# A two-layer hybrid block on one core: the low-rank part of the next RWKV chunk computed in the tail of the chunk before, with reordered norms and a split constants load

## What is computed

```python
h  = rms_norm(x) * norm1_w * (1 + scale) + shift         # scale, shift: silu(c) @ ada_w + ada_b
p  = h @ w_in
# RWKV-7 part; columns of p: r, k, v (512 each), decay and a (64 per direction), gate (128)
p  = p + mu * (neighbour_mean(p) - p)                     # mixing with neighbours in the sequence or grid
g  = sigmoid(gd) @ g_up
kk = k*k_k / norm(k*k_k)
for d in 0, 1:
    w   = -softplus(-(w0[d] + tanh(wd) @ w_up[d])) - 0.5  # low rank: "zw"
    a   = sigmoid(a0[d] + ad @ a_up[d])                   # low rank: "za"
    k_d = k * (1 + (a - 1) * k_a)
o  = forward and backward delta-rule scan(r, w, k_d, v, kk, a)
y1 = (group_norm(o) * lnx_w + lnx_b + sum(r * (k_0 + k_1) * r_k) * v) * g
x += gate1 * (sum of three gated branches) @ w_out        # the others: retention, HGRN2
x += gate2 * (relu(h2 @ w1)**2) @ w2                      # h2: rms_norm(x), scaled and shifted
```

## Time and profile before

| | |
|---|---|
| runs | 2445.9, 2450.27, 2450.76 us (median 2450.27) |
| the profiled execution | 2445.06 us, of which the span from first to last instruction is 2443.3 us |
| mean granted TensorE clock | 0.953 of full speed |
| busy | PE 2190.7 us (90%), DVE 1338.5, ACT 972.3, POOL 421.2 |
| shares of the chain that ended last | PE 76%, DVE 14%, ACT 4%, issue 3%, DMA 1%, POOL 1% |

### The profile page before, as it was taken

One profiled execution on the slowest core, in us unless ns is written; L12 is line 12 of the kernel. 1 busy time (PEld: TensorE's weight loads), 2 busy tenths in 40 slices (PEclk: granted clock), 3 DMA queues, 4 the chain that ended last, 5 costly groups with the idle time before them and its releaser, 6 DMA issues.

```text
span 2443.3 us, 50283 instructions
## 1 busy us (share of the span) xinstructions
PE 2190.7 (90%) x21274; PEld 1849.4 (76%) x21274; DVE 1338.5 (55%) x1913; ACT 972.3 (40%) x1369; POOL 421.2 (17%) x395
## 2 busy tenths in 40 slices
PE   5988889898999899989999988888888889898998
PEld 1655768677778688868888867677776878897998
DVE  3345665656466634454444465476576545566666
ACT  3534232333354323333323346343343364445544
POOL 1001322313134300010000010142232246100000
PEclk8998999999999999989999989899999989898999
DMA  6522412224111123322232223200000022355553
GB/s 248 209 101 76 157 62 106 96 80 157 62 52 61 61 95 99 134 69 95 98 101 95 95 104 132 80 28 28 11 20 27 12 81 70 106 184 173 179 177 128
DMA packets 64447, 241.33 MB, mean 99 GB/s; under 512 B 7136, under 2 KB 8288, under 8 KB 62816
## 3 DMA queue, kind: packets, MB, share of 16 engines
q1 hardware_dynamic: 62064, 218.66, 26.3%
q10 hardware_dynamic: 2160, 19.46, 2.0%
HBM read 231.80 MB, written 6.29 MB: 97 GB/s over the span
## 4 chain that ended last, share of the span: by engine, by line
PE 76%; DVE 14%; ACT 4%; issue 3%; DMA 1%; POOL 1%; DVEq 0%; ACTq 0%; POOLq 0%; SPq 0%
PE psum L392 17%; PE psum L393 16%; PE psum L394 16%; PE psum L447 10%; PE psum L456 2%; PE psum L767 2%; DMA weight_ring<-in_weights 1%; PE psum L703 1%; PE psum L424 1%; PE psum L425 1%; PE psum L485 1%; PE psum L426 1%; DVE work L1155 1%; DVE weight_ring_parts L968 1%; PE psum L434 1%
## 5 line engine op out<-in xcount | busy, mean ns | idle before, releaser
L392 PE MATMUL psum<-normed_high,weights_high 128*128 128x512 f32 (+1 forms) x1592 | 582.9, 366 | 25.5 <-DVE weight_ring_parts L968 12.6
L393 PE MATMUL psum<-normed_low_part,weights_high 128*128 128x512 f32 (+1 forms) x1592 | 566.3, 356 | 0.0
L394 PE MATMUL psum<-normed_high,weight_ring_parts 128*128 128x512 f32 (+1 forms) x1592 | 565.3, 355 | 0.0
L968 DVE TENSOR_TENSOR weight_ring_parts<-weight_ring,weights_high 128x1024 fp32r<-128x1024 f32 (+1 forms) x327 | 411.3, 1258 | 273.5 <-ACT weights_high L1460 266.4
L1460 ACT ACTIVATE weights_high<-weight_ring 128x1024 fp32r<-128x1024 f32 (+1 forms) x327 | 339.9, 1039 | 190.8 <-PE psum L394 136.7
L392 PEld LDWEIGHTS psum<-normed_high,weights_high 128*128 128x128 f32 x1592 | 311.1, 195 | 85.8 <-issue 27.7
L393 PEld LDWEIGHTS psum<-normed_low_part,weights_high 128*128 128x128 f32 x1592 | 311.3, 196 | 41.0 <-issue 3.9
L394 PEld LDWEIGHTS psum<-normed_high,weight_ring_parts 128*128 128x128 f32 x1592 | 310.7, 195 | 40.4
L447 PE MATMUL psum<-work 64*64 64x64 f32 (+1 forms) x7040 | 243.1, 224 | 30.4 <-issue 10.7
L447 PEld LDWEIGHTS psum<-work 64*64 64x64 f32 x7040 | 232.9, 135 | 48.6 <-issue 35.8
L392 PE MATMUL psum<-hidden_high,weights_high 128*128 128x512 f32 (+1 forms) x512 | 172.4, 337 | 3.7 <-DVE hidden_low L1407 3.7
(11 more groups left out here) (233 smaller groups left out, 3534.7 us busy)
## 6 DMA issues: line engine op xcount, KB each, us to landing
weight_ring<-in_weights SPq DMA_DIRECT2D x407, 512.0 KB, 3.5
x_scratch<-work ACTq DMA_DIRECT2D x2, 2048.0 KB, 8.4
weight_ring<-in_weights SPq DMA_DIRECT2D x16, 256.0 KB, 2.7
work<-x_scratch ACTq DMA_DIRECT2D x2, 2048.0 KB, 8.9
work<-in_ret_constants ACTq DMA_DIRECT2D x2, 1152.0 KB, 13.2
work<-in_x ACTq DMA_DIRECT2D x1, 2048.0 KB, 14.0
constants<-in_constants ACTq DMA_DIRECT2D x1, 1317.5 KB, 8.3
work<-in_small_weights ACTq DMA_DIRECT2D x1, 1152.0 KB, 5.2
```

Source lines behind the costliest of these rows:

```text
L392: mm(ps, w[0][:, cols], x[0], start=first, stop=False)
L393: mm(ps, w[0][:, cols], x[1], start=False, stop=False)
L394: return mm(ps, w[1][:, cols], x[0], start=False, stop=last)
L968: tt(ring_r[:, i % RING, o], ring[:, i % RING, o], high[:, n % HIGHS, o].bitcast(F32), ALU.subtract).then_inc(vec_split.sem, vec_split.ste ...
```

## The change

Start and norms:

- the constants load is split: 75 + 512 columns are loaded after x at the start, the other 2048 columns (the masks, a semaphore of their own) after the first norm
- in layer 0 ACT squares x before it copies the modulation rows, PE sums the squares before it makes the modulation columns, and the split of four weights is spread (two before the tiles, one behind tile 1, one behind tile 3)
- in every norm the last square isn't added by DVE: PE sums it in a second accumulating matmul
- in the norms 1 and 2 the high parts of tiles 0 and 1 are written by ACT in an activation of their own instead of by POOL
- the small derived vectors of layer 1 are made in layer 0's last MLP quarter
- `modulation_columns(0, 1)` moves from retention to behind the small projections

RWKV:

- chunk c + 1's low-rank products move into the tail of chunk c on PE, direction 0 in front of the mean's sum and direction 1 between mean and bonus; their sigmoids and exponentials move with them on ACT, their scans and a factors on DVE to between mean and bonus
- `decayed(c + 1)`, five products, ends chunk c on DVE; a times decay comes there from POOL
- chunk 0 has no tail before it: there DVE does `low_rank_parts(0)` and `decayed(0)` before `mix` of k
- the edge columns go from DVE to ACT
- the low part of v's weights moves behind the products with k
- v's projection always uses bank 1 (`second`)

```diff
-                eng.wait_ge(vec_norm.sem, vec_norm.at("squares added", l, which, KT - 1))
-                mm(ps[:, 0:t1 - t0], ones, work[:, TN + 2560:TN + 2560 + t1 - t0], start=True, stop=True).then_inc(
+                eng.wait_ge(vec_norm.sem, vec_norm.at("squares added", l, which, KT - 2))
+                mm(ps[:, 0:t1 - t0], ones, work[:, TN + 2560:TN + 2560 + t1 - t0], start=True, stop=False)
+                eng.wait_ge(act_norm.sem, act_norm.at("square", l, which, KT - 1))
+                mm(ps[:, 0:t1 - t0], ones, work[:, TN + 512:TN + 512 + t1 - t0], start=False, stop=True).then_inc(
...
                 if l == 0:
+                    norm(l, 1)
                     modulation_columns(0, 0)
-                    norm(l, 1)
...
                     if c == 0:
                         eng.wait_ge(act_rwkv.sem, act_rwkv.at("small ready", l))
-                    for d in range(2):
-                        low_rank(c, d)
+                        for d in range(2):
+                            low_rank(c, d)
...
-                    project(big, big_filled, split("rw", l, c, 2), ("rkv", l, c, 2))
+                    project(second, big_filled, split("rw", l, c, 2), ("rkv", l, c, 2))
...
+                    if c < NT - 1:
+                        low_rank(c + 1, 0)
                     eng.wait_ge(vec_rwkv.sem, vec_rwkv.at("o summed", l, c))
                     sum_over(bones, wk(RW_SCR)[:, lo:N], ("mean", l, c), w)
+                    if c < NT - 1:
+                        low_rank(c + 1, 1)
                     eng.wait_ge(vec_rwkv.sem, vec_rwkv.at("bonus terms", l, c))
                     sum_over(bones, wk(RW_KS)[:, lo:N], ("bonus", l, c), w)
...
+                def low_rank_parts(c):
+
+                    for d in range(2):
                         eng.wait_ge(act_rwkv.sem, act_rwkv.at("decay sigmoid", l, c, d))
                         G, sg, msk = wk(RW_D[d] + LT), wk(RW_D[d] + WW), kcol(K_SCAN, N)
...
+                    for d in range(2):
+                        B = RW_D[d]
+                        eng.wait_ge(act_rwkv.sem, act_rwkv.at("a sigmoid", l, c, d))
+                        ts(wk(B + KTI), wk(B + BT), pcol(l, "ka", c), dcol(D_OMKA + c), ALU.mult, ALU.add).then_inc(vec_rwkv.sem, vec_rwkv.step())
...
+                def decayed(c):
+
+                    tt(ks, wk(RW_D[0] + KTI)[:, lo:N], wk(RW_D[1] + KTI)[:, lo:N], ALU.add).then_inc(vec_rwkv.sem, vec_rwkv.step())
...
+                        tt(wk(B + BT), wk(B + BT), wk(B + ABT), ALU.mult).then_inc(vec_rwkv.sem, vec_rwkv.step())
...
+                        tt(wk(B + KTI), wk(B + KTI), wk(B + ABT), ALU.mult).then_inc(vec_rwkv.sem, vec_rwkv.step())
...
+                low_rank_parts(0)
+                decayed(0)
+                for c in range(NT):
...
                         tt(wk(B + KTI), wk(B + KTI), k, ALU.mult).then_inc(vec_rwkv.sem, vec_rwkv.step())
                         eng.wait_ge(vec_rwkv.sem, vec_rwkv.n)
+                    weights_low(split_at["rw", l, c, 2] + 1)
                     mix(c, r, ("mixed", l, c))
...
+                    if c < NT - 1:
+                        low_rank_parts(c + 1)
                     eng.wait_ge(big_filled.sem, big_filled.at("bonus", l, c))
...
-                    weights_low(split_at["rw", l, c, 2] + 4)
+                    if c < NT - 1:
+                        decayed(c + 1)
+                    else:
+                        weights_low(split_at["rw", l, c, 2] + 4)
...
+                        if k < 2:
+                            act(normed_hi[:, k, u0:u1], work[:, o + u0 - t0:o + u1 - t0], ACT.Identity,
...
+                    if c < NT - 1:
+                        tables(SIGMOID)
+                        low_rank(c + 1, 0)
+                        low_rank(c + 1, 1)
+                        tables(LOG_EXP)
                     eng.wait_ge(big_filled.sem, big_filled.at("var", l, c))
...
+                    if c < NT - 1:
+                        decays(c + 1)
+                    else:
+                        tables(SIGMOID)
```

More of the change, by code:

```diff
@@ L284, in banks @@
             return Banks(psum, first, n, width, steps, known, loaded_vectors, held)
-        big, first = banks(0, 4), banks(0, 1)
+        big, first, second = banks(0, 4), banks(0, 1), banks(1, 1)
         wide = banks(2, 1, 2)
@@ L1156, in decay_sums @@
                         eng.wait_ge(vec_rwkv.sem, vec_rwkv.n)
-                    mix(4 + c, k, ("mixed", l, 4 + c))
-                    ts(wk(RW_KK), k, pcol(l, "kk", c), None, ALU.mult).then_inc(vec_rwkv.sem, vec_rwkv.step(("kk raw", l, c)))
-                    eng.wait_ge(vec_rwkv.sem, vec_rwkv.n)
-                    for d in range(2):
-                        decay_sums(d)
                     for d in range(2):
@@ L1464, in _, with squares @@
             split_high = [0]
-            def norm(l, which):
+            def squares(l, which):
                 t0, t1 = (0, N) if which == 1 or l < L - 1 else (NC, N)
@@ L1485, in norm @@
                     eng.wait_ge(act_norm.sem, act_norm.n)
+            def norm(l, which):
+                t0, t1 = (0, N) if which == 1 or l < L - 1 else (NC, N)
+                if which == 3:
+                    t0 = NC
+                n = t1 - t0
                 eng.wait_ge(out_filled.sem, out_filled.at("squares summed", l, which))
@@ L1490, in norm @@
                     return
-                eng.wait_ge(vec_cond.sem, vec_cond.at("vectors derived", l) if which == 1 else vec_cond.at("norm scale", l, "n2"))
+                if (l, which) == (0, 1):
+                    weights_high(2)
+                eng.wait_ge(vec_cond.sem, vec_cond.at("norm scale", l, "n1" if which == 1 else "n2"))
                 ws, sh = (D_WS1, 0) if which == 1 else (D_WS2, 24)
@@ L1501, in norm @@
                         eng.wait_ge(act_norm.sem, act_norm.n)
+                    if (l, which) == (0, 1) and k in (1, 3):
+                        weights_high(3 + k // 2)
                 act_norm.also(("h", l, which))
@@ L1527, in _ @@
                 lo, w, m0 = first_query(l)
-                act(dcol(D_LG, 8), pcol(l, "dec", 0, 8), ACT.Exp).then_inc(act_cond.sem, act_cond.step(("ret decay exp", l)))
-                eng.wait_ge(act_cond.sem, act_cond.n)
                 if l == 0:
+                    act(dcol(D_LG, 8), pcol(l, "dec", 0, 8), ACT.Exp).then_inc(act_cond.sem, act_cond.step(("ret decay exp", l)))
+                    eng.wait_ge(act_cond.sem, act_cond.n)
+                    squares(0, 1)
                     modulation_rows(0, 0)
-                    weights_high(HIGHS)
                 norm(l, 1)
@@ L1663, in _ @@
                     rsqrt(act_rwkv, wk(RW_SQ), big.get("kk norm", l, c), 1.0, "l2", ("kk rms", l, c), ("drained", "kk norm", l, c))
+                    eng.wait_ge(vec_rwkv.sem, vec_rwkv.at("kk ready", l, c))
+                    for d in range(2):
+                        e = 0 if d == 0 else 63
+                        act(chunks(RW_D[d] + KR, 1, e, 128), chunks(RW_KK, 1, e), ACT.Copy).then_inc(act_rwkv.sem, act_rwkv.step(("edges", l, c, d)))
+                        eng.wait_ge(act_rwkv.sem, act_rwkv.n)
                     project(2)
@@ L1839, in _ @@
                             weights_high(split_at["m2", l, q, f] + HIGHS)
+                if l < L - 1:
+                    act(dcol(D_LG, 8), pcol(l + 1, "dec", 0, 8), ACT.Exp).then_inc(act_cond.sem, act_cond.step(("ret decay exp", l + 1)))
+                    eng.wait_ge(act_cond.sem, act_cond.n)
+                    squares(l + 1, 1)
+            squares(L - 1, 3)
             norm(L - 1, 3)
```

112 lines of the change are left out of this document (63 added, 49 removed).

## The result

The changed kernel takes 2429.03 us (median of four runs, 2426.62 to 2431.42) against 2449.69: a ratio of 0.9923, 95% interval 0.9909 to 0.9936. That is faster by 20.7 us where I had forecast 40.

What follows compares the result with a forecast made beforehand. PE, busy 90% of the span, was taken as the bound. Terms 22.3 + 12.3 - 8.9 + 9.6 + 2.7 + 2.3 = 40.3 us off 2445.06 gave 2404.8; with 5.2 for the median, 2410, range 2394 to 2432.

Steps and rivals of the forecast that it cites:

- PE's wait for the edge columns: PE before the first Gram product of each RWKV chunk: 38.3 us in eight waits, forecast gone in chunks 1 to 3.
- new waits for POOL's square: PE's kk sum would wait about 1.4 us in layer 0, 3.8 in layer 1, 6.5 in chunks 0.
- These lose: Chunk 0, low rank and decay before `mix` of k: loss of 4.2 us in layer 0, 4.7 in layer 1.
- The start and the columns: Start: 9.6 us gained by shorter loads and path; modulation columns moved out of retention: 2.7 gained.
- The first L424: At the start, PE would go on at 42.6 us instead of 53.01.
- I count these as equal: Layer 1, chunks 1 to 3: clock cost 2.7 in kk and v against 2.4 gained at Gram products, leaving 12.3 us.
- the product of the bonus terms, which I put into a gap: DVE at level 2: the product fits in a gap and costs nothing; without the gap 0.7 us a chunk, 5.6 in all.
- v and the modulation end at 356.3: Layer 0, chunk 1: PE's own queue sets the first Gram product at 356.3 instead of 361.05, gaining 4.75 us.
- 2.7 us of clock "I take": Layer 0, chunks 1 to 3: full clock at Gram product and transposes gains 2.7 us a chunk, bounds 0 and 2.7.
- Only the waits go, the clock doesn't come back: Rival, 20%: chunks 1 to 3 win 14.2 us in layer 0, 4.5 in layer 1, total 24.4, so 2426.
- The rule against the change: Moved scans beside POOL's square make var about 0.9 us later, at no cost; without slack 5.4 us worse.
- the norms, 2.3: Norms: net gains 0.7 before layer 0's MLP, 0.2 before layer 1, 1.4 before the last MLP, 0 at the end.

Runs made afterwards that it cites:

- the run with k first: Changed kernel, but in chunk 0 DVE mixes k and makes its keys before the scans, a factors and decay products: 2406.81 us, ratio 0.9839 to the kernel before.
- keep_busy: Changed kernel plus PE products whose result is thrown away, filling the wait before the sum of squared keys: ratio 0.9859 to the kernel before.
- bonus_early: Changed kernel, but DVE makes the bonus terms behind the last shifted keys instead of in level 2: ratio 0.9895 to the kernel before.
- the second execution: Second profiled execution of the same changed kernel, nothing edited: span 2433.3 us against 2425.0, ratio 0.9912 to the kernel before.
- v_low_early: Changed kernel, but DVE makes the low part of v's weights in front of the two products with k: ratio 0.9917 to the kernel before.
- layer1_in_head: Changed kernel with k before low rank in chunk 0, and layer 1's low-rank part back in every chunk's head: ratio 0.9902 to the kernel before.
- four_together: Changed kernel with k first in chunk 0, layer 0's modulation before the keys' sum, bonus terms early, POOL rounding all norm tiles: 2407.68 us, ratio 0.9836.

## Why the prediction was right in part

**Right, by its own steps.** PE's wait for the edge columns went (38.3 us). The new waits for POOL's square are 1.49 us in layer 0 (forecast 1.4), 3.3 in layer 1 (3.8), 5.85 and 8.45 in the chunks 0 (6.5). v waits for ACT in the chunks 0. These lose 2.4 to 5.8 and 4.0 us (4.2 and 4.7): in both layers the Gram product comes 6.7 us later behind r's end, as forecast, and the run with k first shows that DVE's order does it. The start and the columns give 10.0 to 11.4 (12.3). The first L424 is at 43.97 instead of 42.6: DVE scales a third tile ahead of the first low part and waits there for ACT, now with four activations a tile, to be done with its buffer; the 1.99 us at 1428.04 are the same wait.

**Wrong: layer 1, "I count these as equal".** The forecast was 12.3 us; 4.2 and 5.2 were measured. I let the clock's cost in kk and v be paid back at the Gram products, so that the whole 4.1 us a chunk would stay. The cost was about right (2.7 forecast, 2.0 to 2.4 by keep_busy), but both sides of it fell short. In front of the Gram product 1.4 us a chunk should have stayed after that cost; it was -0.3, 0.1 and 0.1. In chunk 1, with the ends of chunk 0's state chains laid together, PE sums the keys 0.7 later than forecast, and v then waits for the low part of its weights: 0.70 by its row, 1.09 in keep_busy, where the sum in front of it runs at the full clock. That is a DVE operation that the diff moved in front of a PE product and that my head of DVE had only as work, not as a wait. Behind the Gram product 2.4 to 2.7 should have come back. The Gram products and the transposes behind them did gain 1.8 to 2.8 us, but the whole stretch to the last state product only 0.6, 2.1 and 1.5. Part of what is missing there is the product of the bonus terms, which I put into a gap: the distance from level 2 to level 3 is 5.18 us instead of 4.50 in chunk 2, and with the product moved away (bonus_early) the stretch takes 59.0, 59.1 and 59.2 us instead of 60.6, 59.4 and 59.6.

**Wrong: layer 0, "v and the modulation end at 356.3", and 2.7 us of clock "I take".** With the ends of chunk 0's state chains laid together (9.0 us apart), DVE starts on k at 344.0 (343.0 forecast), PE sums the keys at 348.6 (347.6) and starts the Gram product at 359.6 (356.3). Of these 3.3 us 1.0 is DVE's tail: the mean is 0.7 later, not 0.35, because each half of low rank holds PE 1.9 us and not 1.4, and one decay product takes 1.12 beside POOL. 1.0 is v's low part, and 1.3 is half clock in v (7.1 us instead of 5.8), which chunks 2 and 3 of this execution didn't have. The 2.7 us came at the Gram products of chunks 1 and 2, but the stretch to the last state product was shorter by only 3.0, 1.2 and 0.6 us: 0.45 a chunk went to the bonus terms, and in chunk 3 the clock fell in the body, behind the Gram products. In the second execution it fell in the bodies of chunks 0 to 3. So of the 10.5 us missing in this execution 7.3 lie in front of the Gram products (7.0 of 14.2 won) and 3.3 behind them (4.8 of 8.1).

**Luck: the rival's number.** "Only the waits go, the clock doesn't come back" gives 2426, near the measured 2429, but not for its reasons. It had 14.2 us from the waits in layer 0 and 4.5 in layer 1, all in front of the Gram products. There 7.0 us and nothing came; 4.8 and 4.2, which it left out, came behind them.

**The rule against the change** was weighed rightly where I looked and missed elsewhere. The square of the centred sum took 1.95 us beside the scan. Of the runs, v_low_early shows a like price again (2.01 instead of 1.48), and there it ate half of what v's wait gave. The Trainium skill ("SBUF — State Buffer", § Who interferes with whom) has a DVE instruction with two SBUF inputs and a POOL instruction that reads SBUF exclude each other, which fits both rows and the edge column's 0.17 and 1.12.

**Wrong: the norms, 2.3.** By the ninth product they give -0.1, -1.2 and 1.6 us instead of 0.7, 0.2 and 1.4. The forecast had the two activations on tiles 0 and 1 in its sum, but not DVE's scaling of the third tile behind them, nor that the second sum runs at half clock before layer 1 (1.91 us, so that it costs more than the addition it saves). Rounding by POOL gives back 2 and 3.6 us at the first two.

**Open.** Beyond what the norms' rows explain (-1.3 and 1.6 us), the stage between layer 0's chunk 3 and layer 1 loses 0.8 us and the last one 2 to 3. No run took DVE's longer tail away, so its 1.0 us a chunk is read from rows and not tested; layer1_in_head, which was to test the new wait of layer 1, ran into another. And the single edits' gains don't add up in four_together; the clock's falls differ from run to run by as much as the edits, and no run held them fixed.

## What to carry to other kernels

When a wait of PE is removed, ask where PE stands next, and price the half clock behind that place as a loss of its own (2.0 to 2.4 us a chunk here). Don't count the clock's gain at the old place in full: of 1.8 to 2.8 us at the Gram products 0.6 to 2.1 reached the end of the chunk. Where work is moved ahead on the engine that is late, the step that PE wants first must stay in front of it: the order k, then low rank in chunk 0 was worth 18 to 21 us, as much as the whole change. Where idle time of PE couldn't be filled with work, products that nothing needs kept the clock at 1.00 and made those chunks 1.4 to 2.1 us shorter; that the whole kernel gains by it was measured on the changed kernel and not again with k first.

## What the runs showed of the hardware that I had not expected

- One kernel, profiled twice, had spans of 2425.0 and 2433.3 us, with the clock at half in other places. The last stage, the same code in all kernels but for two norms, took 498.7 to 498.9 us in four profiles, at a mean granted clock of 0.97, and 503.8 to 507.8 in the other thirteen, at 0.94 to 0.95. So a stage that no edit touches differed by 5 us and more between kernels.
- PE was faster with 14 added products (3.36 us) in a wait of 3.3 us than with the wait: 2.4 us less from the keys' sum to the Gram product (11.36 to 8.94).
- An edge column of 8 values per partition took 0.17 us on DVE ahead of POOL's product with b and 1.12 beside it: the row of such a small instruction showed its neighbour's price.
